# Differential attention: one maximum per step, the softmax ratio on GpSimd, one more step of lag

## The reference

```python
s = jnp.einsum('bhcqd,bhckd->bhcqk', qb, k) * scale      # c = 0, 1: two components
s = jnp.where(causal, s, -jnp.inf)
p = jax.nn.softmax(s, axis=-1)
attn = p[:, :, 0] - lam * p[:, :, 1]
o = einsum('bhqk,bhkv->bhqv', attn, v)
o = rms_norm(o, subln_w) * (1.0 - lambda_init)           # over the 128 values of a head
```

## Time and profile before

| what | us |
|---|---|
| time, median of 3 runs (lowest, highest) | 1515.47 (1514.16, 1518.89) |
| the profiled execution's own time | 1516.0 |
| its span in the trace | 1514.3 |
| PE busy | 1458.1 (96%) |
| DVE busy | 945.7 (62%) |
| ACT busy | 692.0 (46%) |
| POOL busy | 80.0 (5%) |
| attention stage, first scores to last value product | 350.07 to about 465.3 |

### The profile page before, as it was taken

How to read it: one execution, slowest core, us unless ns; L and a number is a source line. 1 busy time by engine, 2 the same in 40 slices (tenths; PEclk the granted TensorE clock), 3 DMA queues, 4 the chain that set the end, 5 groups by cost and what they waited for, 6 DMA issues and landing times.

```text
span 1514.3 us, 23149 instructions
## 1 busy us (share of the span) xinstructions
PE 1458.1 (96%) x8808; PEld 1276.3 (84%) x8816; DVE 945.7 (62%) x1650; ACT 692.0 (46%) x1479; POOL 80.0 (5%) x132
## 2 busy tenths in 40 slices
PE   7999999998998999999999989999999999999998
PEld 5889999996668999788989968888888788888886
DVE  5772566637885524612632588887777576557798
ACT  6324222237885424622632465454444464444443
POOL 1000000000000000100000243000000000000012
PEclk9999999999999999999999999999999999999999
DMA  8112111112003620111011242665443598776463
GB/s 317 58 30 56 29 29 29 29 43 70 1 1 88 213 91 29 43 56 43 1 43 42 99 151 71 203 199 203 153 153 120 184 340 296 235 236 194 154 236 125
DMA packets 99437, 177.68 MB, mean 117 GB/s; under 512 B 9600, under 2 KB 42496, under 8 KB 97280
## 3 DMA queue, kind: packets, MB, share of 16 engines
q1 hardware_dynamic: 93632, 152.05, 29.7%
q10 hardware_dynamic: 5696, 24.15, 4.9%
HBM read 138.42 MB, written 37.75 MB: 116 GB/s over the span
## 4 chain that ended last, share of the span: by engine, by line
PE 63%; DVE 4%; issue 2%; ACT 2%; POOL 0%; DMA 0%; POOLq 0%; DVEq 0%; ACTq 0%
PE ps L2029 20%; PE ps L2031 20%; PE ps L2030 20%; PE ps L2324 2%; PE ps L2073 1%; PE ps L2338 0%; DVE wq_l L1772 0%; DVE opl L1613 0%; POOL rms L701 0%; PE ps L2242 0%; DVE mix L1569 0%; DMA raw<-in_w_mk_dram 0%; DVE resid L1645 0%; DVE wl L1280 0%; PE ps L2207 0%
## 5 line engine op out<-in xcount | busy, mean ns | idle before, releaser
L2029 PE MATMUL ps<-wh,oph 128*128 128x256 f32 (+1 forms) x1024 | 294.2, 287 | 3.4 <-issue 1.9
L2030 PE MATMUL ps<-wl,oph 128*128 128x256 f32 (+1 forms) x1024 | 289.6, 283 | 0.0
L2031 PE MATMUL ps<-wh,opl 128*128 128x256 f32 (+1 forms) x1024 | 289.5, 283 | 0.0
L2029 PEld LDWEIGHTS ps<-wh,oph 128*128 128x128 f32 x1024 | 194.9, 190 | 4.3 <-issue 2.4
L2030 PEld LDWEIGHTS ps<-wl,oph 128*128 128x128 f32 x1024 | 195.1, 191 | 0.1
L2031 PEld LDWEIGHTS ps<-wh,opl 128*128 128x128 f32 x1024 | 194.9, 190 | 0.0
L2029 PE MATMUL ps<-d_ring 128*128 128x512 f32 x448 | 175.0, 391 | 2.1 <-DVE d_ring L1903 2.1
L2031 PE MATMUL ps<-d_ring 128*128 128x512 f32 x448 | 175.2, 391 | 0.0
L2030 PE MATMUL ps<-d_ring 128*128 128x512 f32 x448 | 175.0, 391 | 0.0
L1280 DVE TENSOR_TENSOR wl<-raw,wh 128x1024 fp32r<-128x1024 f32 (+1 forms) x60 | 73.2, 1224 | 94.8 <-ACT wh L762 94.0
L701 POOL TENSOR_TENSOR rms<-stat,mhalf 128x1 f32<-128x1 f32 (+2 forms) x59 | 44.5, 762 | 1392.0 <-DVE stat L1284 1370.2
(11 more groups left out here) (338 smaller groups left out, 2953.3 us busy)
## 6 DMA issues: line engine op xcount, KB each, us to landing
right_raw<-in_w_down_dram SPq DMA_DIRECT2D x128, 256.0 KB, 4.0
u_kept_s<-us SPq DMA_DIRECT2D x64, 256.0 KB, 2.4
left_raw<-u_kept_s SPq DMA_DIRECT2D x64, 256.0 KB, 3.0
w_blk<-in_w_up_blocks_dram ACTq DMA_DIRECT2D x14, 1024.0 KB, 5.7
left_raw<-u_kept_a SPq DMA_DIRECT2D x48, 256.0 KB, 3.2
raw<-in_w_in_dram SPq DMA_DIRECT2D x18, 512.0 KB, 3.8
u_kept_a<-u SPq DMA_DIRECT2D x24, 256.0 KB, 2.4
x_in<-in_x_dram SPq DMA_DIRECT2D x8, 512.0 KB, 8.6
```

What stands on the lines that cost most here:

```text
L2029: te.matmul(o, lh, rh, start=first, stop=False)
L2030: te.matmul(o, lh, rl, start=False, stop=False)
L2031: return te.matmul(o, ll, rh, start=False, stop=last)
```

## The change

- `attn_max(n)` makes the maxima of both components in one reduction, once both scores are there; both exponentials wait for it.
- The reciprocal stays on DVE as a part of its own (`attn_rec`); the ratio becomes two multiplications on POOL (`ratio_step`); the combination is a third part and runs one iteration later. DVE's order is now `max(n) rec(n-1) comb(n-2)`.
- `probs` has a third buffer, and everything behind the combination runs one iteration later. PE's order is now `scores(n) T(n-3, 0) PV(n-4) T(n-3, 1)`, ACT's `evac(n-3, 0) O(n-4) evac(n-3, 1) (o_square) exp(n, 0) exp(n, 1)`.
- The squares of the output are no longer taken per step from PSUM with a row sum, but once per token tile over the four heads' 512 columns from SBUF (`o_square`), and DVE sums them (`o_mean`, one reduction more per tile).

The loops run over one iteration more. The diff:

```diff
@@ -271,8 +271,8 @@
...
 vt = at("vt", "V", 0, [P, NT, 512])
-probs = at("probs", "OPH", 0, [P, 2, 2, T])
-probs_t = at("probs_t", "OPH", 16384, [P, 2, NT, P])
+probs = at("probs", "OPH", 0, [P, 3, 2, T])
+probs_t = at("probs_t", "OPH", 24576, [P, 2, NT, P])
 memh = at("memh", "TMP", 0, [P, KD, MEM], F32R)
@@ -364,7 +364,7 @@
...
 recs = small("recs", [P, 4, 2])
-ratio = small("ratio", [P, 2])
+ratio = small("ratio", [P, 4])
 mmax = small("mmax", [P, 2, MH])
@@ -402,7 +402,8 @@
...
 s_done = [sem(f"s_done{c}") for c in range(2)]
-mx_done = [sem(f"mx_done{c}") for c in range(2)]
+mx_done, rec_done, ratio_done = sem("mx_done"), sem("rec_done"), sem("ratio_done")
+o_sq, o_sums = sem("o_sq"), sem("o_sums")
 ex_done = [sem(f"ex_done{c}") for c in range(2)]
@@ -722,7 +723,20 @@
...
         g.tensor_tensor(c22_d[:, j, :], c22_d[:, j, :], gain_a[:, 512:1024], ALU.mult).then_inc(c22_p, 1)
+    def ratio_step(n):
+        pool.wait_ge(rec_done, n + 1)
+        r = ratio[:, n % 4:n % 4 + 1]
+        g.tensor_tensor(r, sums[:, n % 4, 0:1], recs[:, n % 4, 1:2], ALU.mult).then_inc(ratio_done, 1)
+        pool.wait_ge(ratio_done, 2 * n + 1)
+        g.tensor_tensor(r, r, lam[:, 4:5], ALU.mult).then_inc(ratio_done, 1)
+    ratios = 0
     for what in POWS:
+        due = 8 if what == ("mem", 0) else O_STEP[what[1]] + 6 if what[0] == "o" else 0
+        while ratios < min(due, len(ATT_STEPS)):
+            ratio_step(ratios)
+            ratios += 1
         if what == ("down", 0):
@@ -920,12 +934,12 @@
...
         keys = (steps[n][0] + 1) * P
-        act.wait_ge(mx_done[c], n + 1)
-        if n >= 2:
-            act.wait_ge(comb_done, n - 1) if c else act.wait_ge(pt_done, PT_END[n - 2])
+        act.wait_ge(mx_done, n + 1)
+        if n >= 3:
+            act.wait_ge(comb_done, n - 2) if c else act.wait_ge(pt_done, PT_END[n - 3])
         b = score_bank(steps[n][0], c)
         src = ps[:, b:b + 2, :].rearrange("p b k -> p (b k)")
-        s.activation(probs[:, n % 2, c, 0:keys], src[:, 0:keys], ACT.Exp, bias=nmax[:, n % 2, c:c + 1],
+        s.activation(probs[:, n % 3, c, 0:keys], src[:, 0:keys], ACT.Exp, bias=nmax[:, n % 2, c:c + 1],
                      accum_out=sums[:, n % 4, c:c + 1]).then_inc(ex_done[c], 1)
@@ -945,27 +959,35 @@
...
                      ACT.Copy).then_inc(pt_ev, 1)
-    for n in range(NS + 3):
-        if n >= 2 and n - 2 < NS:
-            probs_evac(n - 2, 0)
-        if n == NS + 1:
+    def o_square(k):
+        i = O_COMPLETE[k]
+        m = MIX_TILES.index(i)
+        act.wait_ge(o_ev, k + 1)
+        if m == 0:
+            act.wait_ge(sq_done, 2 * NT)
+        if m >= 2:
+            act.wait_ge(o_sums, m - 1)
+        s.activation(junk[:, 512 * (m % 2):512 * (m % 2) + 512].rearrange("p (h c) -> p h c", h=DH), mix[:, 4:8, i * P:(i + 1) * P],
+                     ACT.Square).then_inc(o_sq, 1)
+    for n in range(NS + 4):
+        if n >= 3 and n - 3 < NS:
+            probs_evac(n - 3, 0)
+        if n == NS + 2:
             mem_hi(0)
-        if n == NS + 2:
+        if n == NS + 3:
             mem_hi(1)
-        if n >= 3:
-            k = n - 3
+        if n >= 4:
+            k = n - 4
             i, h = steps[k]
             act.wait_ge(pv_done, k + 1)
-            o = ps[:, 7, 0:P]
-            s.activation(mix[:, 4 + h, i * P:(i + 1) * P], o, ACT.Copy, scale=recs[:, k % 4, 0:1])
-            if k >= 4:
-                act.wait_ge(o_ev, k - 3)
-            elif k == 0:
-                act.wait_ge(sq_done, 2 * NT)
-            s.activation(junk[:, (k % 4) * P:(k % 4 + 1) * P], o, ACT.Square, scale=recs[:, k % 4, 0:1],
-                         accum_out=stat[:, COL[("o", i)] + h:COL[("o", i)] + h + 1]).then_inc(o_ev, 1)
-        if n >= 2 and n - 2 < NS and steps[n - 2][0] >= 4:
-            probs_evac(n - 2, 1)
+            s.activation(mix[:, 4 + h, i * P:(i + 1) * P], ps[:, 7, 0:P], ACT.Copy,
+                         scale=recs[:, k % 4, 0:1]).then_inc(o_ev, 1)
+        if n >= 3 and n - 3 < NS and steps[n - 3][0] >= 4:
+            probs_evac(n - 3, 1)
+        if n >= 4 and n - 4 in O_COMPLETE:
+            o_square(n - 4)
         if n < NS:
@@ -1536,30 +1558,38 @@
...
     NS = len(steps)
-    def attn_max(n, c):
-        keys = (steps[n][0] + 1) * P
-        dve.wait_ge(s_done[c], n + 1)
+    def attn_max(n):
+        i = steps[n][0]
+        keys = (i + 1) * P
+        dve.wait_ge(s_done[0], n + 1)
+        dve.wait_ge(s_done[1], n + 1)
         if n >= 2:
-            dve.wait_ge(ex_done[c], n - 1)
-        b = score_bank(steps[n][0], c)
-        src = ps[:, b:b + 2, :].rearrange("p b k -> p (b k)")
-        v.tensor_reduce(nmax[:, n % 2, c:c + 1], src[:, 0:keys], AX.X, ALU.max, negate=True).then_inc(mx_done[c], 1)
-    def attn_comb(n):
-        keys = (steps[n][0] + 1) * P
+            dve.wait_ge(ex_done[0], n - 1)
+            dve.wait_ge(ex_done[1], n - 1)
+        src = ps[:, 0:4, :].rearrange("p (c b) k -> p c (b k)", c=2) if i >= 4 else ps[:, 4:6, :]
+        v.tensor_reduce(nmax[:, n % 2, :], src[:, :, 0:keys], AX.X, ALU.max, negate=True).then_inc(mx_done, 1)
+    def attn_rec(n):
         dve.wait_ge(ex_done[0], n + 1)
...
             dve.wait_ge(o_ev, n - 3)
-        after(v.reciprocal(recs[:, n % 4, :], sums[:, n % 4, :]))
-        after(v.scalar_tensor_tensor(ratio[:, n % 2:n % 2 + 1], sums[:, n % 4, 0:1], recs[:, n % 4, 1:2],
-                                     lam[:, 4:5], ALU.mult, ALU.mult))
-        v.scalar_tensor_tensor(probs[:, n % 2, 0, 0:keys], probs[:, n % 2, 1, 0:keys], ratio[:, n % 2:n % 2 + 1],
-                               probs[:, n % 2, 0, 0:keys], ALU.mult, ALU.add).then_inc(comb_done, 1)
+        v.reciprocal(recs[:, n % 4, :], sums[:, n % 4, :]).then_inc(rec_done, 1)
+    def attn_comb(n):
+        keys = (steps[n][0] + 1) * P
+        dve.wait_ge(ratio_done, 2 * n + 2)
+        v.scalar_tensor_tensor(probs[:, n % 3, 0, 0:keys], probs[:, n % 3, 1, 0:keys], ratio[:, n % 4:n % 4 + 1],
+                               probs[:, n % 3, 0, 0:keys], ALU.mult, ALU.add).then_inc(comb_done, 1)
     def o_mean(i):
-        dve.wait_ge(o_ev, O_STEP[i] + 1)
+        m = MIX_TILES.index(i)
+        dve.wait_ge(o_sq, m + 1)
+        c = stat[:, COL[("o", i)]:COL[("o", i)] + DH]
+        v.tensor_reduce(c, junk[:, 512 * (m % 2):512 * (m % 2) + 512].rearrange("p (h c) -> p h c", h=DH), AX.X, ALU.add).then_inc(o_sums, 1)
+        dve.wait_ge(o_sums, m + 1)
         mean(("o", i), P, DH)
@@ -1569,18 +1599,18 @@
...
         ins.then_inc(h_ready, 1)
-    for n in range(NS + 7):
+    for n in range(NS + 8):
         if n < NS:
-            attn_max(n, 0)
+            attn_max(n)
         if 1 <= n <= NS:
-            attn_comb(n - 1)
-        if n < NS:
-            attn_max(n, 1)
+            attn_rec(n - 1)
+        if 2 <= n <= NS + 1:
+            attn_comb(n - 2)
         if n < 3:
...
             y_mean(6 + n)
-        if n == NS + 2:
+        if n == NS + 3:
             for i in range(MT):
@@ -2224,16 +2254,16 @@
...
             ins = te.transpose(ps[:, 6, (b % 4) * P:(b % 4 + 1) * P],
-                               probs[:, k % 2, 0, b * P:(b + 1) * P], ident[:])
+                               probs[:, k % 3, 0, b * P:(b + 1) * P], ident[:])
         ins.then_inc(pt_done, 1)
-    for n in range(NS + 3):
+    for n in range(NS + 4):
         if n < NS:
             scores(n)
-        if 2 <= n < NS + 2:
-            probs_transpose(n - 2, 0)
-        if n >= 3:
-            k = n - 3
+        if 3 <= n < NS + 3:
+            probs_transpose(n - 3, 0)
+        if n >= 4:
+            k = n - 4
             i, h = steps[k]
@@ -2242,8 +2272,8 @@
...
             ins.then_inc(pv_done, 1)
-        if 2 <= n < NS + 2 and steps[n - 2][0] >= 4:
-            probs_transpose(n - 2, 1)
+        if 3 <= n < NS + 3 and steps[n - 3][0] >= 4:
+            probs_transpose(n - 3, 1)
         if n in (NS, NS + 1):
```

## The result

The changed kernel took 1531.75 us (median of 5, 1531.27 to 1535.49) against 1515.47 us: 1.0113 times the time before, 95% interval 1.0097 to 1.0129. The forecast was 1525.0 us, range 1512 to 1531. The direction was right. The rise is 16.3 us where the sum gave 9.5, and the time lies 0.75 us above the range.

What follows compares the result with a forecast made beforehand. PE, busy 96% of the span, was taken as the bound, with a longer ring of waits setting the new pace; 7.2 (pairs) + 0.7 (start) + 1.6 (end) = 9.5 us slower, so 1525.0 us, range 1512 to 1531.

Steps and rivals of the forecast that it cites:

- the sum: Whole kernel: 7.2 for the pairs, 0.7 start, 1.6 end, together 9.5 us slower; this forecast had chance 0.47.
- The ring: Closed waits from one big step's scores to the next: 8.19 us in pairs 7/3, 5.70 in 4/0, formerly 7.78 and 5.12.
- ACT's next instruction is evac(n-2, part 0): Behind exp(n, 1) now stands the big step's copy, which PE's part 1 transposes and scores(n+2) need; formerly a small step's.
- The sum over thirteen pairs: Scores of step 4 to step 30: rings 90.3 us, with extras (squares of memory and output tiles) 94.1 against 86.87, +7.2.
- POOL at 0: The ratio on POOL, priced 2.3 us, fits between rec(n) and comb(n), 2.9 us in 7/3: cost 0, to 0.5 per big step.
- The start: Scores of step 0 to step 4: first exponentials wait for the merged maximum, putting step 4 at 365.0 instead of 364.29, +0.7 us.
- two exponentials (1.09 + 1.11) and about 0.2 to read out the sum put the scores of step 2 at 357.0: In the start, after the merged maximum: scores of step 2 at 357.0 instead of 356.48.
- an alternative: Rival: PE's clock falls at the start, 2 to 4 us more on top of the forecast, 1528 us; chance 0.18.
- Longer than any wait of the stage before: The clock rival's reason: PE stands about 3.5 us before step 2 and 2.7 before the first transposes.
- The end: Scores of step 30 to the end of the splits, formerly 22.31 us: +1.6 us, from 0 to 4.
- The reductions: In the end, o_mean adds a 512-column reduction (0.7 us) and a wait to each of two serial chains: +1.5 us.
- the one iteration more of draining is about what PE waited there before: In the end, the extra drain iteration about equals PE's former waiting (busy 17.64 of 22.31 us): +0.1 us.

Runs made afterwards that it cites:

- e3: The kernel before with nothing but the lag: third probability buffer, transposes, value products and combination one iteration later; 1533.94 us, ratio 1.0114.
- e12: The changed kernel with one edit: on DVE comb(n-2) stands before max(n) instead of behind it; 1532.22 us, ratio 1.0114.
- e9: The changed kernel with a big step's part 1 transposed behind the scores that waited for it, ACT and DVE reordered, fourth probs buffer; 1522.33 us, ratio 1.0051.
- e5: The changed kernel with two maxima again, one per component, each releasing its own exponential; 1531.46 us, ratio 1.0103.
- e6: The changed kernel with the maximum over only the first half of each component's keys, waits unchanged; 1529.79 us, ratio 1.0092.
- e1: The changed kernel with unread identity products in PE's waits of the first and last steps and before the memory projection; 1531.06 us, ratio 1.0096.
- e7: The kernel before with nothing but the squares once per tile (o_square, reduction in o_mean); 1523.51 us, ratio 1.0052.
- e11: e10 with identity products on PE where it would wait, in the start, the last steps and before the memory projection; 1526.95 us, ratio 1.0085.
- e10: e9 with the squares of the output per step, as before the change; 1525.36 us, ratio 1.0075.

## Why the forecast was right in kind and too small in size

**The ring, right.** The point "ACT's next instruction is evac(n-2, part 0)" decides. The sum over thirteen pairs was 94.1 with extras against 95.25 measured; 1.0 of the difference is the low clock in the first pair. The pairs that the trace shows one by one, the waits in them and e3 (the lag alone has the whole rise) show it; e12 (DVE's order has none of it) and e9 (6.6 us less, with the link cut among other things) agree. e5 and e6 show that the maximum is no part of the price.

**POOL at 0, right.** The ratio is never waited for in the changed kernel's pairs: DVE's combination at 382.31 starts on the heels of the reciprocal. The ratio itself was priced too dear: the forecast had 2.3 us for both multiplications, and they took 1.4 (382.47 to 383.88), the first 1.15 us when it started 0.16 us behind a combination, and 0.19 when DVE was idle (e9 at the end of a maximum). The Trainium skill, "SBUF — State Buffer", section "Who interferes with whom", has it that either side excludes the other; the trace shows DVE's combination holding up POOL by about 1 us. It doesn't show the reverse: at 462.90 POOL began a power that took 1.01 us, and a combination on DVE that began meanwhile, at 463.24, took 0.33 us, as one of 128 columns does elsewhere. POOL's times are rough, so this is a hint and no proof.

**The start, mis-sized: 0.7, measured 3.35.** The step "two exponentials (1.09 + 1.11) and about 0.2 to read out the sum put the scores of step 2 at 357.0" held but for the stage's later begin and an extra 0.2; what failed was leaving PE's clock at 1.00. The scores of step 2 took 1.8 us more and the transposes 0.4 (the 1.0 more of the scores of step 4 stands in the first pair). I had given that a chance of 0.18 as an alternative and its cost, 2 to 4 us, correctly; it should have had more weight, though not for the reason that it gave. "Longer than any wait of the stage before" is no condition (and the second of the two waits, 2.7 us, wasn't longer than the 2.94 of before): behind the unchanged 2.94 us five other kernels ran the same scores at low clock, and the one profile of the kernel before, from which the term was read, did not. The Trainium skill, "TensorE: Matmul & The Clock Gate", Part 1, says that the default state is the throttled one and that activity releases it; the stretch at 0.52 behind a wait of 3.61 us agrees. e12, whose start has the same work, shows 17.56 us, so +3.3 again; e5 and e6, whose maxima are ready earlier, 16.32 and 15.37, and e1 with its fillers 15.86.

**The end, mis-sized: 1.6, measured 4.2, and 3.3 behind it that had no term.** The reductions are there as forecast. The step "the one iteration more of draining is about what PE waited there before", +0.1, failed: PE ran 6.9 us of that drain at a clock of 0.52, 1.9 us longer in ten value products (2.35 for 1.28) and one tile's transposes (1.91 for 1.05) alone, and I had stopped the ledger at the splits, though the splits' delay goes on into the loading of the weights. Over kernels: from the scores of step 30 to the output projection's first power before took 130.0 us, the changed kernel 137.5, the same end in e5, e6 and e12 133.5 to 134.8. The lag alone (e3) makes 132.3, the tile squares alone (e7) 134.1, and with the link cut, tile squares against step squares are 134.6 to 132.3. So 3.5 to 4.8 us are the usual price of the change there, and the rest of the 7.5 is of this one execution.

**How the median comes together.** 3.3 in the start, 8.4 in the pairs, 3.5 to 4.8 in the end: 15.2 to 16.5, against 16.3 measured. The same can be read from whole executions. Of the 37 of the kernel before that ran beside the experiments, the twelve with a mean granted clock of 0.996 or more took 1512.4 to 1515.4 us, the five at 0.989 to 0.991 took 1518.5 to 1522.2. The changed kernel's five are all at 0.988 to 0.991, and the three of them at 0.989 to 0.991 took 1531.3 to 1531.8. At like clock the change so costs 9 to 13 us, around the 9.5 of the sum; the rest of the 16.3, an estimate of some 5 us, goes with the clock. This is a comparison of executions and doesn't say in which stage the clock was low; and e1, at 0.993 to 0.995, was still at 1527.7 to 1531.8, so the clock that the fillers gave back wasn't time given back.

**What stays open.** What decides whether the clock falls in the start, and how much of the low clock's cost a better order could save. In one execution each, holding it at 1.00 gave 1.7 us in the start and 1.1 in the first pair (e1 against the changed kernel), nothing in the start and 1.6 in the first pair (e11 against e10), and no median shows it. The split of the end between its serial chain and the clock rests on single profiles that differ by 1 to 3 us.

## What to carry to other kernels

When a pipeline written out by hand gets one more step of lag, work out again what now stands behind the long instruction on each in-order engine; a lag of one with alternating big and small steps exchanges the two, and here a copy on which PE's next scores hang came behind 2.2 us of exponentials. Before relieving an engine, ask whether the ring goes through it: 5.9 us less of DVE's work and 7.2 less of ACT's were worth nothing, and e9's order, with the transposes of part 1 behind the scores, was worth 9. One profile isn't enough to take PE's clock from: the 2.94 us wait of the start ended at full clock in the one of the kernel before and at low clock in five others. Read the clock of several executions, and put what low clock costs behind a wait of PE into the range at least. And follow a delay through the next stage's loads before closing the ledger.

## What the runs showed of the hardware

A multiplication of one column on POOL took 0.19 us with DVE idle (378.49 in e9) and 1.15 us when it started just behind a combination of 1024 columns on DVE with two inputs in SBUF; behind one of 640 columns it took 0.75, behind one of 512 it took 0.62. It ended 0.05 us behind DVE's instruction, which kept its length. And the low clock cost nothing where PE had a wait to come, and its full share where it had none. In e10's start the scores of step 2 took 2.54 us and in e11's 1.99, and both reached step 4 after 14.97 us; in the pair behind it, where PE of e10 was busy for all of 9.32 us, the clock was 0.82 and the pair 1.63 us longer than e11's at 1.00. With 7 us at 0.52 in its start the changed kernel was there 1.7 us slower than e1, whose clock was full. The Trainium skill, "TensorE: Matmul & The Clock Gate", section "Terms", reckons the penalty as the throttled time times one minus the ratio, so half of it here, for the changed kernel's 7 us an estimate of some 3.5 us; the trace shows half of that, as PE was waiting in part of the stretch anyway. For e10's pair it is 0.18 of 9.32 us, an estimate of 1.7, and the 1.63 agree.
